# A hybrid attention layer on eight cores: where the input gain is applied, which queue loads and casts, and which engine shares the elementwise work

## The reference

```python
def rms_norm(x, g):
    y = x * lax.rsqrt(jnp.mean(x * x, axis=-1, keepdims=True) + EPS)
    return y * g

h = rms_norm(x, g_in)
(c_q, c_kv, k_pe, z_mla, q_swa, k_swa, v_swa, z_swa, q_mem, z_mem) = split_cols(h @ w_in, IN_SIZES)
# IN_SIZES = 512, 256, 64, 1024, 512, 128, 128, 512, 512, 512
y_mla = mla_attention(c_q, c_kv, k_pe, g_q, g_kv, w_uq, w_ukv, cos, sin) * silu(z_mla)   # 8 heads, all earlier 64-row chunks
y_swa = swa_attention(q_swa, k_swa, v_swa, sinks, rel_table) * silu(z_swa)               # window of 128, sinks, bias
y_mem = memory_attention(q_mem, rms_norm(mem, g_mem), w_mem_kv) * silu(z_mem)            # 256 memory rows
h = x + concat([y_mla, y_swa, y_mem]) @ w_out
return rms_norm(h, norm_final)
```

## Time and profile before

| | us |
|---|---|
| median of 3 runs | 842.4 (842.06 to 845.37) |
| profiled execution | 846.9 |
| its span on core 0, the slowest | 845.3 |
| cores 0 to 7 | 845.3, 833.0, 767.5, 819.4, 842.3, 835.9, 768.2, 819.6 |
| core 0, busy: TensorE, VectorE, ScalarE, GpSimd | 696.5, 517.2, 321.2, 20.9 |

### The profile page before, as it was taken

How to read it: one execution, slowest core, us unless ns; L and a number is a source line. 1 busy time by engine, 2 the same in 40 slices (tenths; PEclk the granted TensorE clock), 3 DMA queues, 4 the chain that set the end, 5 groups by cost and what they waited for, 6 DMA issues and landing times.

```text
span 845.3 us, 10585 instructions; the slowest of 8 cores (767.5 to 845.3 us)
## 1 busy us (share of the span) xinstructions
PE 696.5 (82%) x3514; PEld 320.5 (38%) x3514; DVE 517.2 (61%) x702; ACT 321.2 (38%) x502; POOL 20.9 (2%) x69
## 2 busy tenths in 40 slices
PE   0353999999898799998899877867668799999993
PEld 0121555555343134444444333323223344444441
DVE  0552686988444678657567497985868763433332
ACT  1214611201532666553255455335346531222221
POOL 4000000000000000000000000001000000000000
PEclk9985999999999599999999999889879999999997
DMA  8999420853020217620001000001805734534312
GB/s 268 271 289 241 73 100 7 297 195 100 1 98 8 95 51 208 185 100 0 1 1 51 1 0 2 1 0 24 177 0 114 261 76 125 196 128 175 125 56 98
DMA packets 14422, 88.69 MB, mean 105 GB/s; under 512 B 1676, under 2 KB 1808, under 8 KB 6552
## 3 DMA queue, kind: packets, MB, share of 16 engines
q1 hardware_dynamic: 10968, 65.38, 22.1%
q0 software_dynamic: 3392, 22.55, 13.2%
HBM read 94.21 MB, written 11.53 MB: 125 GB/s over the span
## 4 chain that ended last, share of the span: by engine, by line
PE 62%; DVE 11%; ACT 10%; DMA 7%; issue 7%; another core or an unknown queue 2%; POOL 1%; ACTq 0%; DVEq 0%; POOLq 0%; SPq 0%
PE psd L596 62%; DMA ws_r<-wkv 5%; ACT ze_r L576 3%; ACT pmb_r L576 3%; DMA out<-xo_r 2%; DVE z_r L579 2%; DVE qv_r L579 2%; DVE gA_r L579 1%; ACT K_r L576 1%; ACT rim_r L576 1%; DVE xo_r L583 1%; DVE w_r L579 1%; DVE Qn_r L590 1%; DVE oc_r L579 1%
## 5 line engine op out<-in xcount | busy, mean ns | idle before, releaser
L596 PE MATMUL psd<-x_r,w_r 128*128 128x512 bf16 (+1 forms) x1344 | 277.4, 366 | 9.8 <-DVE z_r L579 7.4
L596 PEld LDWEIGHTS psd<-x_r,w_r 128*128 128x128 bf16 x1344 | 131.0, 99 | 151.6 <-issue 25.4
L596 PE MATMUL psd<-x_r,wkv_r 128*128 128x512 bf16 (+3 forms) x240 | 51.6, 392 | 55.2 <-DVE wkv_r L1491 40.5
L579 DVE TENSOR_TENSOR w_r<-st_r,gv_r 128x1024 bf16<-128x1024 f32 x72 | 86.1, 1217 | 8.5 <-PE psd L596 5.2
L576 ACT ACTIVATE pmb_r<-psd 128x768 bf16<-128x768 f32 (+2 forms) x80 | 67.4, 874 | 59.0 <-PE psd L596 55.1
L596 PE MATMUL psd<-wo_r,gA_r 128*128 128x512 bf16 x352 | 83.2, 379 | 2.3 <-DVE xo_r L579 2.3
L576 ACT ACTIVATE junk_r<-xo_r 128x512 f32<-128x512 f32 x44 | 27.7, 629 | 110.6 <-DVE xo_r L579 105.4
L579 DVE TENSOR_TENSOR xo_r<-psd,xo_r 128x512 f32<-128x512 f32 x44 | 30.3, 689 | 59.1 <-PE psd L596 57.0
L576 ACT ACTIVATE ze_r<-z_r 128x512 f32<-128x512 f32 (+1 forms) x48 | 28.1, 590 | 93.0 <-DVE z_r L579 66.4
L576 ACT ACTIVATE ze_r<-ze_r 128x512 f32<-128x512 f32 (+1 forms) x96 | 55.6, 590 | 6.2
L596 PEld LDWEIGHTS psd<-x_r,wkv_r 128*128 128x128 bf16 (+1 forms) x240 | 23.4, 106 | 82.2 <-issue 65.0
...
## 6 DMA issues: line engine op xcount, KB each, us to landing
...
out<-xo_r SPq DMA_DIRECT2D x22, 512.0 KB, 3.3
st_r<-wmk SPq DMA_DIRECT2D x8, 1024.0 KB, 12.5
...
x_r<-xu POOLq DMA_DIRECT2D x4, 512.0 KB, 21.7
...
```

The costliest lines, as they stand in the source:

```text
L579: self.P.op(eng, lambda e: e.tensor_tensor(out=out, in0=a, in1=b, op=op), reads, writes, (n / (2 if fast else 1) + 151) / 960.0)
L596: ins = e.matmul(out, lhsT=l, rhs=r, start=s0, stop=s1, skip_group_check=True)
```

## The change

- **Gain.** `norm_in` is multiplied into a core's own features (`scale_own`, 16 instructions of one block by unit) instead of into the weights. Own units come in float32 on SP (`load_own`, four loads of up to 1 MiB each) and are written as bf16 by VectorE, ScalarE or GpSimd. The memory rows get `norm_mem` in the same way. Earlier tokens' units still come cast by the POOL queue; for these the kv weights are scaled once more into a second copy (`rest_weights`; roles 1 to 3 only). The squares are taken from the unscaled features as before.
- **Weights.** `w` tiles and kv weights are cast to bf16 by their loads, all on the POOL queue. `fold_w` and `ws` are gone: no weight instruction on VectorE for role 0.
- **Order of loads.** Gains and features of unit 0 on SP, kv weights on POOL, are issued ahead of the branch at addresses that all roles share (`pin`). Then w tiles one and two, unit 1, w tiles three and four; the memory rows; the constants of the window attention come only before its queries.
- **Branch.** Two numbers, two comparisons on every path.
- **Rotary part.** The rows are swapped by small SBUF to SBUF DMAs on SP; products and sum then work on all rows and may run on GpSimd. `sin` has its sign on the other half.
- **Shared work.** The planner may put gate products, the first level of the probability sums, the final products, three of four square sums and the rotary products on GpSimd as well as VectorE, the diagonal memsets on VectorE as well as GpSimd, and copies out of PSUM of q, k, v and the attention output on ScalarE as well as VectorE. GpSimd waits for its own last instruction where the rows worked on differ.
- **Planner.** New DMA costs with the two queues sharing the wires, space reserved for loads ahead, 14 space limits tried instead of 6. Roles 2 and 3 begin own projections without waiting until all own units have their kv. The division of tokens is unchanged.

```diff
+    def load_own(self, u, q):
+        T = self.T[u]
+        pin = PIN_X + q * 8192 if u == 0 else None
+        t, p = self.P.new("xs", [128, 4, T], F32, pin)
+        o = self.xoff[u] + q * 512 * T
+        self.P.dma("sp", t[:, :, :].rearrange("p k t -> p (k t)"),
+                   self.dr["xu"][o:o + 512 * T].rearrange("(p c) -> p c", c=4 * T), writes=[p], mb=T / 512.0, what="xs")
+        self.xs[u, q] = (t, p)
+
+    def scale_own(self, u, q):
+        st, sp = self.xs[u, q]
+        x, parts = self.x[u]
+        for k in range(4):
+            kc = 4 * q + k
+            self.gain(x[:, kc, :], st[:, k, :], self.g_in[:, kc:kc + 1], [sp], [parts[q]], self.T[u])
...
+    def gain(self, out, in_, g, reads, writes, n):
+        fn = lambda e: e.tensor_scalar(out=out, in0=in_, scalar1=g, scalar2=None, op0=ALU.mult)
+        self.P.op({"dve": (fn, (n / 2 + 151) / 960.0), "pool": (fn, n * 1.4 / 960 + 0.1),
+                   "act": (lambda e: e.activation(out=out, in_=in_, func=AF.Copy, scale=g), 0.29 + n / 1200.0)},
+                  None, reads + [self.gvp], writes)
...
     def load_w(self):
...
-        st, sp = self.P.new("st", [128, 16, 128], F32)
-        self.P.dma("sp", st[:, :, :].rearrange("p a b -> p (a b)"), src, writes=[sp], what="w")
-        self.staged.append((st, sp, g))
-
-    def fold_w(self):
...
-        self.tt(ALU.mult, w[:, ks, :], st[:, ks, :], g[:, ks].unsqueeze(2).to_broadcast([128, 8, 128]),
-                [sp, self.gvp], [wp], 1024)
+        w, wp = self.P.new("w", [128, 16, 128], BF16)
+        self.P.dma("pool", w[:, :, :].rearrange("p a b -> p (a b)"), src, writes=[wp], what="w")
+        self.ready.append((w, wp))
...
     def own_stream(self):
-        while not self.own_done:
+        while not self.own_done and self.role < 2:
             yield None
...
+        for q in range(4):
+            self.load_own(0, q)
+            if q == 0:
+                P.dma("sp", gv[:, :], self.dr["gv"][:, :], writes=[self.gvp], mb=.02, what="gv")
+            P.dma("pool", bw.t[:, 4 * q:4 * q + 4, :].rearrange("p a b -> p (a b)"),
+                  self.dr["wkv"][q * 262144:q * 262144 + 262144].rearrange("(p c) -> p c", c=2048), writes=[wp[q]], what="wkv")
...
+        self.load_w()
+        self.load_w()
+        if self.no > 1:
+            self.fetch(1)
+        self.load_w()
+        self.load_w()
...
         def qp(u):
...
-            self.tt(ALU.mult, a[:, :], self.pf(b, 0, T), cs[:, 0, us], [self.PS[b], csp], [ap], T)
+            self.cp(a[:, :], self.pf(b, 0, T), [self.PS[b]], [ap], T, "both")
             for g in range(4):
                 i0 = 32 * (g ^ 1)
-                self.tt(ALU.mult, v[32 * g:32 * g + 32, :], self.pf(b, 0, T, i0, i0 + 32), cs[i0:i0 + 32, 1, us],
-                        [self.PS[b], csp], [vp], T)
-            self.tt(ALU.add, self.Q[p][2][:, us], a[:, :], v[:, :], [ap, vp], [self.Q[p][3][u]], T)
+                P.dma("sp", v[32 * g:32 * g + 32, :], a[i0:i0 + 32, :], reads=[ap], writes=[vp], mb=.06, what="swap")
+            self.tt(ALU.mult, a[:, :], a[:, :], cs[:, 0, us], [ap, csp], [ap], T, False, True)
+            self.tt(ALU.mult, v[:, :], v[:, :], cs[:, 1, us], [vp, csp], [vp], T, False, True)
+            self.tt(ALU.add, self.Q[p][2][:, us], a[:, :], v[:, :], [ap, vp], [self.Q[p][3][u]], T, False, True)
...
     def tt(self, op, out, a, b, reads, writes, n, fast=False, pool=False, rows=None):
+        fn = lambda e: e.tensor_tensor(out=out, in0=a, in1=b, op=op)
+        eng = {"dve": (fn, (n / (2 if fast else 1) + 151) / 960.0)}
+        if pool:
+            eng["pool"] = (fn, n * 2.2 / 960 + 0.1)
...
-                self.tt(ALU.add, t[:, :, :], x[:, :, 0:cols], y[:, :, 0:cols], [xp, yp], [tp], 2 * cols, True)
+                self.tt(ALU.add, t[:, :, :], x[:, :, 0:cols], y[:, :, 0:cols], [xp, yp], [tp], 2 * cols, True, True)
...
-                P.op("pool", lambda e, o=o: e.memset(pb[64:128, :, o:o + 64], 0.0), [], [pbp], 0.2)
+                fn = lambda e, o=o: e.memset(pb[64:128, :, o:o + 64], 0.0)
+                P.op({"pool": (fn, 0.2), "dve": (fn, 0.25)}, None, [], [pbp], rows=(64, 128))
...
     def body(e, eng):
+        n = FIRST.get(eng, 0)
+        progs[0].replay(eng, e, 0, n)
+        e.reg_load(hi, role_d[0:1, 0:1])
+        e.reg_load(lo, role_d[0:1, 1:2])
+        with e.If_eq(hi, 0):
+            with e.If_eq(lo, 0):
+                progs[0].replay(eng, e, n, None)
...
```

370 lines of the change are left out of this document (199 added, 171 removed).

## The result

The changed kernel takes 863.9 us (863.48 to 868.28, three runs) where the kernel before takes 842.4 (842.06 to 845.37): ratio 1.026, 95% interval 1.020 to 1.032. The forecast was 817 with a range of 797 to 836, so its sign was wrong. What came is the number of the slow rival, 862, which had a chance of 0.09.

What follows compares the result with a forecast made beforehand. Core 0 was taken as the bound, with 149 us of TensorE idle time in four places. Terms 17 + 4 + 6 - 2 = 25 us off the profiled 846.9 gave 821.9, on the median's scale 817; range 797 to 836.

Steps and rivals of the forecast that it cites:

- the slow rival: GpSimd's elementwise work holds VectorE's two-operand products, memsets or weight issue; 0.3 us per moved operation, 862 us, chance 0.09.
- the four places of idle time: TensorE on core 0 idles 58 us up to 77.1, 30 from 208 to 510, 42.6 in latent attention, 15 behind 820.
- Part 1: Head: reordered loads let TensorE start unit 1 at about 58 instead of 77.2 us; 17 us gained, ends 2 and 26.
- Constants move behind: Head: constants are loaded after features, kv weights and first w tiles; no cost was counted for it.
- if VectorE does all: Head: scaling the last quarter of x1 adds four instructions at 0.48 us, 1.9 us in all on VectorE.
- the stall for unit 2: Head: unit 2 loaded at 72.4, scaled by 74, needed at 79; a stall of 2 us, ends 0 and 11.
- Part 3: Rotary part by DMA swaps of 1 to 4 us each, far ahead of use: cost nothing, gain counted in latent attention.
- the loads ahead of the branch: Start of the programs: issuing five and six loads early saves core 0 under 1 us; it matters for core 1.
- Part 2: VectorE's weight scaling, 86.1 us, goes; of TensorE's 8.0 us of waits for z, 4 us are gained.
- Part 4: Latent attention: relief of VectorE by freely placed copies, sums and products gains 6 us, ends 0 and 20.
- Part 5: About 156 operations on core 0 may move to GpSimd; cost 2 us, ends 0 and 47.
- few stand right before TensorE: Of the operations that may move to GpSimd, few come right before TensorE's need, so 2 us of cost was taken.

Runs made afterwards that it cites:

- b_copies: Kernel before, with only the copies out of accumulator banks (queries, keys, values, attention output) free to go to ScalarE or VectorE: 824.0 us, ratio 0.978.
- a_npold: Changed kernel without elementwise work on GpSimd, with the earlier one-register chain of comparisons and no loads ahead of the branch: 814.0 us, ratio 0.964.
- a_nopool: Changed kernel without elementwise work on GpSimd (products, sums and scaling no longer offered to it; memsets stay): 814.6 us.
- a_idc: Changed kernel with the identity table cast to bf16 by its load on GpSimd's queue instead of by VectorE: 863.5 us.
- a_noswap: Changed kernel with the four partial rotary products of the kernel before instead of row swaps by DMA: 844.8 us, ratio to before 1.002.
- a_both: Changed kernel with neither elementwise work on GpSimd nor row swaps by DMA: 835.0 us, ratio 0.991.

## Why the prediction was wrong

**What bounds it** held: core 0, the four places of idle time, and the rule that the core which ends next limits a gain (b_copies and a_npold stop at role 3).

**Part 1, the head: 17 us forecast, 12.8 us lost.** The price of the loads held as far as x1: its last quarter landed at 54.6 us, forecast 55.7. Five steps failed. First, "Constants move behind" was costed at nothing. The identity table's cast was still first in VectorE's program, so the same stall that I had found in the kernel before (a small load behind megabytes) stayed: first matmul at 33.38 us, not before 20. Second, scaling was put at 1.9 us from x1's landing to unit 1, "if VectorE does all":

```profile
69.00 9.71 PE L646 MATMUL psd<-x_r,wkv_r 128*128 128x512 bf16 x31 [11.53 <-POOL x_r L637]
```

It took 14.4 us, with ten of unit 1's sixteen scalings on GpSimd at 1.7 us each. In a_nopool, with none there, it was still 10.6 us; what sets these is open. a_idc, without the cast, shows the forecast times (15.65 and 57.75), the second by luck: x1 landed at 48.0, 7.7 us before its forecast, and unit 1 began 9.8 us after it. Third, the stall for unit 2: I took 2 us, ends 0 and 11, from 1.5 MiB of slack. Eleven w tiles, not four, landed ahead of it, it was whole at 97.1 us instead of 72.4, and the DMA share was 0.96 to 1.04 from 6 to 98 us. Fourth, the keys' rotary swaps, put at nothing in Part 3, stand in the head: TensorE's 8.2 us above, and a head of 114.8 us in a_noswap. Fifth, the loads ahead of the branch were put at under 1 us of gain and cost 4.6, with the new branch 11.4. That the head is bound by all bytes that are asked for in it, so that moving one load to the front moves the wait, fits a_idc (unit 1 19 us earlier than before, the first own-weight matmul still 3.7 us later), but is not shown.

**Part 2, weight scaling: 4 us forecast, none seen.** The failed step is that scalings standing ahead on VectorE made TensorE wait for z. They are gone, and the wait for z in a_nopool and a_npold is 10.3 and 10.4 us, against 8.0 before. From memory weights to up-projection a_npold takes 367.1 us against 370.6 before, but b_copies, which still scales every weight tile, takes 364.9. No run takes the weight scaling alone away. In the changed kernel the wait for z is 17.4 us; the 7 us above a_nopool come with GpSimd's share, by what path is not shown.

**Part 3, swaps: nothing forecast.** The step "the query part is used one head pair later, so nothing" looked for who needs the data. It should have asked what stands behind the waiting instruction on its engine: a memset and a product, and TensorE 14.5 us behind them; the first window keys another 8.2. I had put 1 to 4 us for a swap, which holds when the wires are free (median 2.0 us); beside two loads of output weights four took 27. With GpSimd out of it, 5.6 us in the head are left (a_nopool against a_both), and no cost elsewhere is seen beyond the spread of plans.

**Part 4, latent attention: 6 us forecast, ends 0 and 20; measured 36.6 and 34.0** for the free choice of engine for copies alone. The mechanism was named ("copies that either engine may take"), its size was not worked out. The rows held it: 36 copies of 1.13 us on an engine that is 77% busy, beside one at 49%, and each copy keeps a bank. I halved the idle time as the upper end, as if the rest were a fixed chain; the wait for exponentials fell from 31.7 to 10.2 us.

**Part 5, GpSimd: 2 us forecast, ends 0 and 47; measured 49.** The bounds for a single product were right: a 1024-column one took 2.5 us, near the 2.3 estimated from the Trainium skill (GPSIMD Engine Reference, Performance versus the Vector engine). The failed step is "few stand right before TensorE": distance from TensorE does not matter when each moved instruction also holds VectorE. How the 49 us divide between this hold and GpSimd's own length and queue, which TensorE's waits name with 11.5 and 14.5 us, is not separated. The slow rival named this hold, priced it at 0.3 us each and gave 862. That the number was met is luck: it kept 27 us of gains, where the runs show 44.2 gained and 12.7 and 50.6 lost (next paragraph). For the rival stood the Trainium skill's rule and a VectorE busy 77% with two-operand sums; against it only an argument. A chance of 0.09 was not what these rows said.

**The sum on core 0**, by runs: 845.3, less 44.2 (copies, b_copies), plus 12.7 (branch and early loads, a_nopool against a_npold), plus 50.6 (GpSimd, after against a_nopool) is 864.4, and the span is 861.9; so all that is left of the change is worth 2.5 us. These are differences of single plans; the first and the last are no better known than to some 20 us in the total, and are firm only in the stage where the edit lies.

Of the signs listed, right were: no scaling of w on VectorE, VectorE near 400 (383.9), GpSimd at 80 to 250 (199.3), core 0 the slowest. Wrong: the first matmul, unit 1 (69.0), role 3 (822, not below 810); and of the signs named against it three came: a second stall of 5.3 us before 90, TensorE's waits for GpSimd at 27 us, sums of 1.75 us.
